# The 64 by 64 inverse of a delta rule: 64-column blocks against 32-column diagonal blocks with the corner last

## The reference, cut to what matters

```python
A = jnp.where(strict, jnp.einsum("bnhid,bnhjd->bnhij", kb, kc) * gamma, 0.0)   # 64 x 64, strictly lower
T = lax.linalg.triangular_solve(A + eye, eye, left_side=True, lower=True)      # (I + A)^-1
u = jnp.einsum("bnhij,bnhje->bnhie", T, vc * bc[..., None])
w = jnp.einsum("bnhij,bnhjd->bnhid", T, kb * eG)
# then a scan over the 8 chunks: v_new = u - w S;  o = qg S + att v_new;  S = S * dl + kd^T v_new
```

## Time and profile before

| | |
|---|---|
| median of 3 runs | 2515.05 us (2512.92 to 2515.93) |
| span of the profiled execution | 2513.4 us |
| what the median has beyond that span | 1.7 us |
| PE busy | 2479.0 us, 99% of the span |
| DVE busy / ACT busy | 1622.7 us (65%) / 1209.6 us (48%) |
| the delta rule's part of the second block | about 1590 to 1950 us of the span |

### The profile page before, as it was taken

One profiled execution on the slowest core, in us unless ns is written; L12 is line 12 of the kernel. 1 busy time (PEld: TensorE's weight loads), 2 busy tenths in 40 slices (PEclk: granted clock), 3 DMA queues, 4 the chain that ended last, 5 costly groups with the idle time before them and its releaser, 6 DMA issues.

```text
span 2513.4 us, 37708 instructions
## 1 busy us (share of the span) xinstructions
PE 2479.0 (99%) x15346; PEld 2065.3 (82%) x15346; DVE 1622.7 (65%) x2583; ACT 1209.6 (48%) x2027; POOL 75.9 (3%) x114
## 2 busy tenths in 40 slices
PE   9999999999999999999999999999999999999998
PEld 7999888887878778878999888777776788888887
DVE  6888348866765555348887257766877655677733
ACT  6555334765546465245555246544333454444421
POOL 0111000000000000000110000000000000000000
PEclk9999999999999999999999999999999999999999
DMA  5675332222212222233775322211111112333232
GB/s 166 179 181 156 109 100 85 84 76 76 83 65 72 76 68 80 89 101 93 176 185 149 100 90 96 76 43 35 43 43 51 59 59 84 99 94 101 88 101 72
DMA packets 80525, 237.82 MB, mean 95 GB/s; under 512 B 8928, under 2 KB 10976, under 8 KB 80352
## 3 DMA queue, kind: packets, MB, share of 16 engines
q1 hardware_dynamic: 68832, 213.56, 26.5%
q0 software_dynamic: 10080, 18.35, 4.7%
q10 hardware_dynamic: 1440, 3.49, 0.4%
HBM read 233.27 MB, written 2.10 MB: 94 GB/s over the span
## 4 chain that ended last, share of the span: by engine, by line
PE 93%; DVE 4%; ACT 1%; DMA 1%; issue 1%; SPq 0%; ACTq 0%; DVEq 0%
PE bank L2311 22%; PE bank L2313 21%; PE bank L2312 21%; PE bank L2325 4%; PE bank L2327 4%; PE bank L2326 4%; PE bank L2580 2%; PE bank L2505 1%; PE bank L2411 1%; PE bank L2513 1%; PE bank L2499 1%; PE bank L2676 1%; PE bank L2486 1%; DVE hl L3094 1%; PE bank L2340 0%
## 5 line engine op out<-in xcount | busy, mean ns | idle before, releaser
L2311 PE MATMUL bank<-uR,hl 128*128 128x512 f32 x1684 | 683.4, 406 | 5.1 <-DVE uR L3105 3.2
L3094 DVE TENSOR_TENSOR hl<-raw,hl 128x1024 fp32r<-128x1024 f32 (+2 forms) x325 | 385.8, 1190 | 445.1 <-ACT hl L2725 443.8
L2313 PE MATMUL bank<-uR,hl 128*128 128x512 f32 x1684 | 658.0, 391 | 0.0
L2312 PE MATMUL bank<-uR,hl 128*128 128x512 f32 x1684 | 657.5, 390 | 0.0
L2725 ACT CAST hl<-raw 128x1024 fp32r<-128x1024 f32 (+2 forms) x325 | 329.8, 1020 | 204.8 <-PE bank L2313 196.1
L2311 PEld LDWEIGHTS bank<-uR,hl 128*128 128x128 f32 x1684 | 317.0, 188 | 93.9 <-issue 23.6
L2313 PEld LDWEIGHTS bank<-uR,hl 128*128 128x128 f32 x1684 | 316.7, 188 | 68.3
L2312 PEld LDWEIGHTS bank<-uR,hl 128*128 128x128 f32 x1684 | 317.3, 188 | 66.5 <-issue 6.0
L3088 DVE TENSOR_TENSOR hl<-raw,hl 128x1024 fp32r<-128x1024 f32 (+1 forms) x142 | 150.7, 1075 | 35.6 <-ACT hl L2721 32.4
L2325 PE MATMUL bank<-sum,hl 128*128 128x256 f32 x560 | 158.8, 284 | 2.5 <-DVE fA L3272 2.5
L2326 PE MATMUL bank<-sum,hl 128*128 128x256 f32 x560 | 158.5, 283 | 0.0
(11 more groups left out here) (521 smaller groups left out, 4337.4 us busy)
## 6 DMA issues: line engine op xcount, KB each, us to landing
raw<-in_win SPq DMA_DIRECT2D x147, 512.0 KB, 3.5
raw<-in_w SPq DMA_DIRECT2D x44, 512.0 KB, 3.5
raw<-in_w1u SPq DMA_DIRECT2D x54, 256.0 KB, 3.0
raw<-in_w2u SPq DMA_DIRECT2D x51, 256.0 KB, 3.1
raw<-in_w1g SPq DMA_DIRECT2D x22, 512.0 KB, 4.8
raw<-in_w2g SPq DMA_DIRECT2D x22, 512.0 KB, 4.5
raw<-in_w1d SPq DMA_DIRECT2D x16, 512.0 KB, 3.5
raw<-in_wssd SPq DMA_DIRECT2D x16, 512.0 KB, 3.6
```

The costliest lines, as they stand in the source:

```text
L2311: e.matmul(s.bank[:, :], h[:, 0, w], hi, start=s.first and q == 0, stop=False)
L2312: e.matmul(s.bank[:, :], h[:, 0, w], lo, start=False, stop=False)
L2313: i = e.matmul(s.bank[:, :], h[:, 1, w], hi, start=False, stop=s.last and q == n - 1)
L3094: e.tensor_tensor(h[:, 1, w], x[:, w], h[:, 0, w].bitcast(F), ALU.subtract).then_inc(*sig("dve_split.lo", s, i))
```

## The change

The inverse is now made for the 32 by 32 diagonal blocks only, by levels 1 to 4, and the corner block (rows 32 to 63 by columns 0 to 31 of T) is joined at the end. The diagonal blocks of a chunk lie side by side in partitions: 4 blocks of 32 partitions (2 heads x 2 halves) x 8 chunks of 32 columns, which is 128 x 256. A page of 512 columns holds two such arrays: DU is D (the diagonal blocks of AT) and U, TY is T and Y, Ak the two masked copies. A product is 32x32 weights against 32 moving columns, 32 products make one `blocks32`, and they go to four tiles on the diagonal of the array. The planner's `COSTS` for these steps are changed with it, and one page fewer is taken.

```diff
+QUARTER = tuple(slice(32 * i, 32 * i + 32) for i in range(4))
+FIRST, SECOND = slice(0, 256), slice(256, 512)
...
-    if k == "gdn_fold" and s["lev"] == 5:
-        return [("PE", 1.07), ("DVE", 0.69, "dve_gdn.U")]
...
-    "gdn_seed": [("DVE", 1.4, "dve_gdn.U0"), ("DVE", 0.66, "dve_gdn.A", 0), ("DVE", 0.66, "dve_gdn.A", 1)],
-    "gdn_seed_turn": [("PE", 1.15), ("ACT", 0.6, "act_gdn.T")],
-    "gdn_level": [("PE", 1.07, "pe_gdn.Y"), ("ACT", 0.6, "act_gdn.Y"), ("DVE", 0.5, "dve_gdn.mask")],
-    "gdn_fold": [("PE", 2.14, "pe_gdn.fold"), ("DVE", 0.69, "dve_gdn.T"), ("DVE", 0.69, "dve_gdn.U")],
+    "gdn_seed": [("DVE", 1.6, "dve_gdn.U0"), ("DVE", 0.4, "dve_gdn.A", 0), ("DVE", 0.4, "dve_gdn.A", 1)],
+    "gdn_seed_turn": [("PE", 0.6), ("ACT", 0.4, "act_gdn.T")],
+    "gdn_level": [("PE", 0.6, "pe_gdn.Y"), ("ACT", 0.4, "act_gdn.Y"), ("DVE", 0.3, "dve_gdn.mask")],
+    "gdn_fold": [("PE", 1.2, "pe_gdn.fold"), ("DVE", 0.42, "dve_gdn.T"), ("DVE", 0.42, "dve_gdn.U")],
+    "gdn_corner": [("PE", 0.6), ("ACT", 0.8, "act_gdn.corner")],
+    "gdn_join": [("PE", 0.7), ("ACT", 0.8, "act_gdn.join")],
...
-        for lev in range(1, 6):
+        for lev in range(1, 5):
...
-        AT.release(s_mask)
+        yield from ready(tt, banks=1)
+        b = SB.take()
+        s6 = step("gdn_corner", AT=AT, DU=DU, TY=TY, U=U, tt=tt, ut=ut, free=wY, b=b)
...
+        yield from ready(("act_gdn.corner", s6), ut, banks=1)
+        b = SB.take()
+        s7 = step("gdn_join", DU=DU, TY=TY, U=U, ut=ut, s=s6, b=b)
```

TensorE's program:

```diff
-        def blocks64(b, x, y):
+        def blocks32(b, x, y):
             for c in range(C8):
-                at = slice(c * 64, c * 64 + 64)
-                for r in HALF:
+                at = slice(c * 32, c * 32 + 32)
+                for r in QUARTER:
                     i = e.matmul(b[r, at], x[r, at], y[r, at], start=True, stop=True)
...
+        def gdn_corner(s):
+            after(*s.tt, *s.b.after)
+            for c in range(C8):
+                at = slice(c * 32, c * 32 + 32)
+                for i in range(2):
+                    top, low = QUARTER[2 * i], QUARTER[2 * i + 1]
+                    t = e.matmul(s.b[low, at], s.AT[top, 64 * c + 32:64 * c + 64], s.TY[top, at], start=True, stop=True)
...
+        def gdn_join(s):
+            go.wait_ge(*on("act_gdn.corner", s.s))
+            after(*s.ut, *s.b.after)
+            U, Y = s.DU[:, SECOND], s.TY[:, SECOND]
+            for c in range(C8):
+                at = slice(c * 32, c * 32 + 32)
+                for i in range(2):
+                    top, low = QUARTER[2 * i], QUARTER[2 * i + 1]
+                    e.matmul(s.b[top, at], Y[low, at], U[low, at], start=True, stop=True)
+                    t = e.matmul(s.b[low, at], con[1][low, low], U[low, at], start=True, stop=True)
```

ScalarE's program:

```diff
+        def gdn_corner(s):
+            go.wait_ge(*on("pe_gdn.corner", s))
+            after(*s.free)
+            for i in range(2):
+                low = QUARTER[2 * i + 1]
+                x = e.copy(s.TY[low, SECOND], s.b[low, FIRST])
...
+        def gdn_join(s):
+            h = CCOLS["halves"][0]
+            after(*s.ut, *s.U.after)
+            activate(v8(s.U)[:, :, 0:32], c32(s.DU[:, SECOND]), ACT.Copy, scale=con[1][:, h:h + 1])
+            go.wait_ge(*on("pe_gdn.join", s))
+            activate(v8(s.U)[:, :, 32:64], c32(s.b[:, FIRST]), ACT.Copy,
+                     scale=con[1][:, h + 2:h + 3]).then_inc(*sig("act_gdn.join", s))
```

VectorE's program, in `gdn_seed`:

```diff
-            e.tensor_tensor(v8(s.U), v8(s.AT), chunks8(con[1][:, lv:lv + 64]), ALU.mult).then_inc(*sig("dve_gdn.Um", s))
+            D, U = c32(s.DU[:, FIRST]), c32(s.DU[:, SECOND])
+            e.tensor_scalar(D, v8(s.AT)[:, :, 0:32], con[1][:, h:h + 1], None, ALU.mult).then_inc(*sig("dve_gdn.D0", s))
+            go.wait_ge(*on("dve_gdn.D0", s))
+            e.scalar_tensor_tensor(out=D, in0=v8(s.AT)[:, :, 32:64], scalar=con[1][:, h + 1:h + 2], in1=D, op0=ALU.mult,
+                                   op1=ALU.add).then_inc(*sig("dve_gdn.D", s))
+            go.wait_ge(*on("dve_gdn.D", s))
+            e.tensor_tensor(U, D, chunks8(con[1][:, lv:lv + 32]), ALU.mult).then_inc(*sig("dve_gdn.Um", s))
```

More of the change, by code:

```diff
@@ L1920, in gdn_prep @@
         At = [("dve_gdn.A", s4, 0), ("dve_gdn.A", s4, 1)]
         yield
-        wY = list(Y.after)
-        for lev in range(1, 6):
-            A = (Ak, Ak2)[(lev + 1) % 2]
-            yield from ready(At[(lev + 1) % 2], Tm, banks=1)
+        wY = []
+        for lev in range(1, 5):
+            yield from ready(At[(lev + 1) % 2], tt, banks=1)
             b = SB.take()
-            s6 = step("gdn_level", lev=lev, A=A, at=At[(lev + 1) % 2], AT=AT, Tm=Tm, tt=list(Tm.t), Y=Y, free=wY, b=b)
+            s6 = step("gdn_level", lev=lev, A=Ak, at=At[(lev + 1) % 2], DU=DU, TY=TY, tt=tt, free=wY, b=b)
@@ L1928, in gdn_prep @@
             b.release(("act_gdn.Y", s6))
[L1929 to L1938, removed]
@@ L1939, in gdn_prep @@
-            b.release(*U.t)
+            if lev < 3:
+                At[(lev + 1) % 2] = ("dve_gdn.mask", s6)
+            yield from ready(("act_gdn.Y", s6), ut, banks=2)
+            b, b2 = SB.take(), SB.take()
+            s7 = step("gdn_fold", DU=DU, TY=TY, ut=ut, tt=tt, s=s6, b=b, b2=b2)
+            tt, ut = [("dve_gdn.T", s7)], [("dve_gdn.U", s7)]
+            b2.release(*tt)
+            b.release(*ut)
             wY = [("pe_gdn.fold", s7)]
             yield
-        Tm.release(("pe_gdn.Y", s6))
@@ L1947, in gdn_prep @@
+        U.t = [("act_gdn.join", s7)]
+        b.release(*U.t)
+        DU.release(*U.t)
+        TY.release(*U.t)
+        yield
         yield from ready(U, *vb, banks=2)
@@ L2585, in gdn_seed_turn @@
             after(*s.b.after)
+            U = s.DU[:, SECOND]
             for c in range(C8):
[L2587 to L2589 removed]
+                at = slice(c * 32, c * 32 + 32)
+                for r in QUARTER:
+                    i = e.matmul(s.b[r, at], U[r, at], con[1][r, r], start=True, stop=True)
             i.then_inc(*sig("pe_gdn.seed", s))
@@ L3002, in gdn_seed_turn @@
             go.wait_ge(*on("pe_gdn.seed", s))
-            after(*s.Tm.after)
-            e.copy(s.Tm[:, :], s.b[:, :]).then_inc(*sig("act_gdn.T", s))
+            after(*s.TY.after)
+            e.copy(s.TY[:, FIRST], s.b[:, FIRST]).then_inc(*sig("act_gdn.T", s))
         def gdn_level(s):
@@ L3883, in constants @@
     put(b, "incl64", p <= f)
-    put(b, "id64", p == f)
-    for lev in range(6):
+    put(b, "halves", np.concatenate([p < 32, p >= 32, np.where(p < 32, -1, 1)], axis=1))
+    p, f = p % 32, np.arange(32)[None, :]
+    put(b, "id32", p == f)
+    for lev in range(5):
         n = 1 << lev
         m = (p // (2 * n) == f // (2 * n)) & (f // n % 2 == 1) & (p // n % 2 == 0)
-        at = CCOLS["level"][0] + 64 * lev
-        b[:, at:at + 64] = m
+        at = CCOLS["level"][0] + 32 * lev
+        b[:, at:at + 32] = m
     return a, b
```

66 lines of the change are left out of this document (36 added, 30 removed).

## The result

The changed kernel takes **2528.59 us** (2528.22 to 2529.37, four runs) against 2514.5 us in the same session: ratio **1.006 [1.0046, 1.0074]**, 14 us slower. I had forecast 2495. The span is 2526.4 us (2513.4 before). The time lies in my range, but on the other side of no change. Of all executions here three were disturbed (6229 and 7541 us for the changed kernel with half the instructions, 2549 us for the kernel before) and stand in no median or ratio.

A forecast was written before the change was run, and what follows sets the result against it. PE was taken to bound the kernel: 2513.4 us of span, less 25.8 for shorter bursts, plus 4.5 and 1 given back, makes 2493.1; the median lies 1.7 above, so 2495 us, range 2485 to 2545.

The forecast's parts named there:

- What bounds the kernel: Whole kernel: PE, busy for 99% of the span, sets the time; other engines count only where PE waits for them.
- The bursts: Inverse's products on PE: 44 bursts fall from 62.4 to 36.6 us at 7.8 ns a record, a gain of 25.8 us.
- the paired starts: Inside a burst before: matmuls start in pairs, one per tile, some 60 ns between pairs, at most 15 ns within the last.
- The third rival: PE as a whole can't start or be fed records at the forecast pace: 22 ns a record, 2541 us; chance 0.25.
- A dense cycle: Where scan and inverse alternate without a projection: a cycle of 4.85 us gains about 0.95, not 1.29, as DVE is late.
- The waits for copies and DVE: Dense stretches and seed: about 13 cycles give back 4.5 us, the seed's extra hops 1 us; corner and join copies nothing.
- DVE takes over: Delta rule's part: three of four pairs gain nothing because DVE decides, 2507 us; chance 0.10.
- Floor per tile: Products' tiles: a 32-column record takes as long as one of 64, 58.1 ns a tile, 2515 us; chance 0.18.
- Engine-wide pace: Inverse's records on PE: one price per record on the engine, not the tile; loss from 15.0 ns, 2541 us; chance 0.25.
- 25 ns between starts: Trainium skill's price for PE matmuls: starts never closer than about 25 ns, whatever the size; 99.4 us sum, 37 us slower.
- the rule on small sizes: Trainium skill on PE matmuls: about 60 cycles overhead, free size 1 as slow as 60; by it the sum is about zero.
- The other criterion of the text: Sign that the forecast is wrong: the bursts are short and the span doesn't follow.

The follow-up runs named there:

- half the instructions: Changed kernel, with one matmul in levels and folds for two chunks at once (64 moving columns, odd chunks with wrong weights): 2511.44 us, ratio 0.9994.
- other order: Changed kernel with the main stream's projections reordered to lie between most bursts and ROOM2 4 instead of 6: 2504.66 us, ratio 0.9969.

## Why the prediction was wrong

**What bounds the kernel: right.** PE bounds it before and after (92% of the chain).

**The bursts: right.** The tile's own pace, taken from the paired starts, gave 7.8 ns a record; it is 8.8. The gain on PE's work was forecast at 25.8 and is 23.8 us.

**The failed step: a burst's pace was taken as the pace of the whole.** The step "I take 7.8, since the paired starts are the nearest row to it" priced 3712 records by how fast the engine executes those that it has, and I asked nowhere what brings them. The third rival had it in words ("can't start or be fed records at that pace", "a pair of close starts may come from a queue that had filled"), but I worked it out as one price on every record, and looked for it in the length of a burst. In fact both prices hold: 8.8 ns for records that are there, and 27 to 31 ns over a long run of them. Where projections of 0.23 us a matmul lie between, the changed kernel has only one break (0.27 us, at 1640.9); the others come where scan and inverse alternate. A dense cycle of 192 records was to take 4.85 - 0.95 = 3.9 us, 20 ns a record: faster than the supply gives them, and all of these numbers stood in my text. The page's third part had the queue too, 122 packets and 2.00 MB, over 30692 instructions of PE. By equal orders, half the instructions give back 17 us (new costs), 23.2 (old costs) and 12.7 (other order), of which 3.1, 1.8 and 7.5 us are less work on PE, and the rest idle time and clock. The shortest distance before, 4.82 us between two packets, wouldn't have given the limit, but it would have shown that the 128 records in 2.6 us which such a cycle asks for were outside anything in this trace.

**The clock: named, and priced at nothing.** I wrote that less PE work in the dense stretches "could bring one more such fall" and took 3 us either way. It was +27.2 us, the largest term of all, and more than the whole gain. With supply no limit and the order nearly as before it was 3.1 us (9.2 against 6.2). Without the breaks alone it is 20.7 us instead of 33.4, without the new costs alone 24.0. So most of the clock's cost is a consequence of the breaks and of the new order together. What makes each single fall isn't shown: some come behind waits for DVE. The Trainium skill, "TensorE: Matmul & The Clock Gate", section "What's actually happening", says that TensorE runs at a low clock when it isn't kept busy. The trace agrees in direction only: 0.59 where PE was idle for 2.7 of 20 us, with short bursts and breaks, but 1.00 in the other order, where it was idle for 2.0.

**The new `COSTS`: priced at 0 with 3 us either way, cost 8 us and more.** This is the second step that failed. It is 2528.59 against 2520.43 with the old ones, and where the supply is no limit 2511.44 against 2497.22, 14 us. The two terms don't simply add: with both taken away 31.4 us are gone, of the 33.6 between forecast and result. Most of it is clock: 9.4 us where the span differs by 8.3, and 11.5 where it differs by 18.1 and there are no breaks. That they pack the bursts closer together, between projections held back until six pages are free, is likely but not shown; the breaks didn't get fewer without them.

**The waits for copies and DVE: about right where they can be seen.** I gave back 4.5 + 1 us. In the kernel after, idle time ended by ACT and DVE before the inverse's matmuls didn't grow (some 6 us against 7.7), since breaks stood in its place. With neither breaks nor the new costs, the whole idle time grew by 4.6 us (39.0 against 34.4).

**The sum, if the supply were no limit,** is what the run with half the instructions and the old costs tests: span 2494.7 us against the 2493.1 forecast, 2497.2 against 2495. The terms were -26.4 work (25.8 forecast), +4.6 idle (5.5), +3.1 clock (0). That they fit so well is in part luck: the work includes what fewer records save, and the run has the old costs, so it leaves out the term of the new ones. It isn't a version that could be used, as it computes the odd chunks with the wrong weights, but it shows that the supply and the order by the new costs together are what stood between forecast and result.

**The rivals.** DVE takes over: no. Floor per tile: no (0.68 us a burst). Engine-wide pace: its sign and its mechanism of feeding were right, its size wasn't (2541 worked out), and its test, "1.8 and over" for a burst of 64, would have missed it. The 25 ns between starts that the prediction cites don't hold across the four tiles, which took 8.8 ns a record; and where the rule on small sizes made PE's gain about zero, it was 23.8 us. The other criterion of the text caught it: the bursts are short and the span doesn't follow.

**Open:** what exactly brings the clock down. Much the same idle time (37.5 and 41.1 us) goes with 4.8 us in one order and 15.5 in another, and the breaks with it are the same (8.9 and 9.0). Also open is where the gain of the change in pair 0 alone went. No version of the exact computation with fewer instructions was run, so what the supply costs is read from kernels that also do a little less work.

## What to carry to other kernels

Before work is split into many small instructions, count instructions per microsecond in the densest stretch: here 256 of PE (128 matmuls with their weight loads) came every 3.3 to 4 us, and where the bursts asked for more than that, under some 27 ns a matmul, the engine starved, however fast it executed. The order has to be planned anew with such a change: it cost 14 us as planned, and gained 13 in another order against the kernel before in that order, 8.6 against the kernel before in its own. That short bursts pay wherever full-width matmuls stand between them isn't shown; in pair 0 alone they didn't. A hole can cost more than its length, since the clock may fall with it (8.2 us of breaks; without them the clock cost 12.7 us less in the same order), so read the granted clock by stretches before a gain in a thin stretch is believed.

## What the runs showed of the hardware

- Four 32x32 tiles beside each other execute float32 records of 32 columns at 8.8 ns a record (0.56 us for 64), 35 ns a tile, against 58 ns for 64 columns on a 64x64 tile before; so a record of 32 columns has no floor at the price of 64.
- Instructions of PE come in 16 KB packets of 256; the closest two were 3.26 us apart in the changed kernel and 3.5 to 4.0 us in a burst that did nothing but ask for them.
- One matmul of 64 columns in place of two of 32 needs half the instructions for the same columns; PE's work fell by 3.1, 1.8 and 7.5 us in three orders.
- In the same stretch and with nearly as many records (x599 and x610), the granted clock was 0.59 without projections between the bursts and 1.00 with them.
